# A ring of streamed expert weights: one matrix's slabs issued from ScalarE's queue instead of SyncE's

## Chip, cores and metric

One Trainium2 chip, one core. The metric is the device time of one execution in microseconds (us). Engines are named as in the profile: PE (TensorE), DVE (VectorE), ACT (ScalarE), POOL (GpSimd), SP (SyncE); an engine's name with q behind it is its sequencer.

## What is computed

The program computes two transformer blocks on 512 tokens of width 1024, all in float32. The first block (differential attention, a gated delta rule in both directions, then a mixture of experts) is followed by a second one of another kind. The change lies in the experts alone, which the reference gives as:

```python
def expert_choice_ffn(h, w_router, w_gate, w_up, w_down):   # 16 experts, width 2048
    cap = CAP_FACTOR * s // N_EXPERTS                        # 64 tokens for each expert
    aff = softmax(einsum('bsd,de->bse', h, w_router))
    top_val, top_idx = lax.top_k(swapaxes(aff, 1, 2), cap)
    xs = h[top_idx]
    gt = einsum('becd,edf->becf', xs, w_gate)
    up = einsum('becd,edf->becf', xs, w_up)
    ye = einsum('becf,efd->becd', silu(gt) * up, w_down)
    ye = ye * top_val[..., None]
    # scatter: every row of ye is added to its token's row of the output
```

Each of the three matrices of an expert has 2 million float32 values, 8 MB; the 16 experts' weights are 403 MB, each read once.

## The kernel before, in words

The weights of the experts go through a ring of 8 buffers (RING), each of 128 partitions by 4096 values, 2 MB. A load of one buffer is a slab. An expert x has PER = 12 slabs, numbered r = 12x to 12x + 11: four of w_gate, four of w_up, four of w_down ("down slabs"). Slab r goes to buffer r % 8. PE counts every slab that it has finished on the semaphore E7["used"]; slab r may be issued once used has reached r - 7, that is when slab r - 8 is finished. SP walks over all 192 slabs in order, waits for that count and issues one DMA for each (L1843 to L1854 with the helper expert_slab, whose plain issue is L1817; the slabs 8 to 11 go in two halves, L1814, and the last one, 191, in four quarters, L1821). All DMAs of the kernel are issued by SP.

PE runs the experts in order, two to a pair (L2081 to L2116). For each it does the gate slabs (wide(GB, ...), matmuls at L2048), in the second expert of a pair (odd x) four transposes (L2092), the up slabs (wide(UB, ...), L2048 too), the gather of the next pair's tokens (L2022), then turn (transposes, L2057) and two down slabs, turn and two more (down, L2077 and L2078). After the second expert of a pair comes the scatter: 8 products (L2115) that DVE adds to X (L2378). In the trace a slab is 16 matmul records, in pairs that run side by side on two halves of the array.

ACT does for each expert: two Silus of the gate's banks, which wait for used to reach 12x + 4 (L2186, L2187), the copy of the gathered tokens (L2178), and the two copies behind turn (L2192). DVE multiplies Silu by up (L2362), and copies the expert's output (L2367, L2368). Behind the stage, SP loads some constants for the next one (L1857 to L1864), each behind the buffer that it overwrites.

The loop of SP, cut:

```python
for r in range(NE * PER):
    ...
    elif r >= NR + 4:
        sp.wait_ge(E7["used"], r - NR + 1)
    expert_slab(sp, r)
```

Of the kernel before, what the change touches and what calls it, by code (L numbers as in the profile page):

```python
# [27 lines left out]
NE = 16  # L28
# [82 lines left out]
def build(nc, io):  # L111
    ctx = ExitStack()
    counts = {}
    with ctx:
# [5 lines left out]
        def sem(name):  # L120

            return cleared.pop(0) if cleared else ctx.enter_context(nc.semaphore(name))
# [87 lines left out]
        def load_slab(eng, slot, src, cols):  # L210

            k = src.shape[0] // P
            dst = SLB[slot][:, 0:k * cols].rearrange("p (k n) -> p k n", k=k)
            eng.dma_start(dst, src.rearrange("(k p) n -> p k n", p=P)).then_inc(slab_in[slot], 16)
            slab_n[slot] += 16
            return slab_in[slot], slab_n[slot]
# [938 lines left out]
        with nc.Block() as block:  # L1155
# [609 lines left out]
            E7 = {n: sem("e_" + n) for n in names}  # L1765
# [5 lines left out]
            NR = len(RING)  # L1771
            PER = 12
# [25 lines left out]
            def free_ring(eng, buf):  # L1798
                eng.wait_ge(E7["used"], max(r for r in range(NE * PER) if RING[r % NR] is buf) + 1)

            def expert_slab(eng, r):

                x, part = r // PER, r % PER
                if part < 8:
                    w, rows, f0 = (w_gate, w_up)[part // 4], 256, part % 4 * 256
                else:
                    w, rows, f0 = w_down, 512, DOWN[part - 8] * 512
                src = w[x, f0:f0 + rows, :].rearrange("(p k) n -> p (k n)", p=P)
                if NR <= r < NR + 4:

                    for k in range(2):
                        eng.wait_ge(*((E7["used"], r - NR + 1) if k else (E7["half"], r - NR + 1)))
                        cols = slice(k * 2 * D, (k + 1) * 2 * D)
                        eng.dma_start(RING[r % NR][:, cols], src[:, cols]).then_inc(ring_in[r % NR], 16)  # L1814
                    return
                if r < NE * PER - 1:
                    eng.dma_start(RING[r % NR][:, :], src).then_inc(ring_in[r % NR], 16)  # L1817
                    return

                for k in range(4):  # L1820
                    eng.dma_start(RING[r % NR][:, k * D:(k + 1) * D], src[:, k * D:(k + 1) * D]).then_inc(slab_in[4 + k], 16)  # L1821
                    slab_n[4 + k] += 16
                    quarter_in.append((slab_in[4 + k], slab_n[4 + k]))
# [3 lines left out]
            @block.sync  # L1827
            def _(sp):
                halves = lambda src, n: src[:, n * 512:(n + 1) * 512]
                sp.wait_ge(E4["o_done"], 2 * len(PAIRS))  # L1830
                sp.dma_start(wr, io["w_router"][0].rearrange("(k p) e -> p k e", p=P)).then_inc(E6["wr"], 16)
                for slot, src in ((5, halves(w_in[:, GATE_G:GATE_G + D], 1)), (6, halves(wpg, 0)), (4, halves(wpg, 1)),
                                  (0, halves(wo, 0)), (1, halves(wo, 1))):
                    if slot == 4:
                        sp.wait_ge(E4["sq4"], HEADS)
                    elif slot == 0:
                        sp.wait_ge(E4["og_ready"], HEADS)
                    elif slot == 1:
                        sp.wait_ge(q_done, 2 * SEVEN)
                    w5.append((slot, load_slab(sp, slot, src, 512)))  # L1840
                sp.dma_start(x3, io["x"][0].rearrange("(t p) d -> p t d", p=P)).then_inc(x_in, 16)

                for r in range(NE * PER):  # L1843
                    if r == 0:
                        sp.wait_ge(q_done, NQ * SEVEN)
                    elif r == 2:
                        sp.dma_start(n2row, io["norm2_w"].to_broadcast([P, D])).then_inc(E6["n2"], 16)
                    elif r == 4:
                        sp.wait_ge(merge5, KD)
                    elif r == 5:  # L1850
                        sp.wait_ge(m5, 2 * NT)
# [4 lines that stand above are left out]
                free_ring(sp, R[1])  # L1856
                sp.dma_start(nfrow, io["norm_f_w"].unsqueeze(0).to_broadcast([P, D])).then_inc(consts_in, 16)  # L1857
                sp.dma_start(onehot, io["table"][0:32, T_BUCKET:T_BUCKET + REL]).then_inc(consts_in, 16)
                sp.dma_start(rb, io["rel_bias_2"]).then_inc(consts_in, 16)
                sp.dma_start(kvrow, io["kv_norm_g_2"].to_broadcast([P, P])).then_inc(consts_in, 16)  # L1860
                sp.dma_start(w_uk, io["w_uk_2"][0].rearrange("h d r -> d h r")).then_inc(consts_in, 16)
                free_ring(sp, R[3])
                for to, c, n in ((0, A_CKV, P), (P, A_IK, 64), (P + 64, A_IW, 8)):
                    sp.dma_start(wm[:, :, to:to + n], w2[:, c:c + n].rearrange("(k p) n -> p k n", p=P)).then_inc(consts_in, 16)  # L1864
# [254 lines left out]
            def _(act):  # L2119
# [56 lines left out]
                def gathered(q, hf):  # L2176
                    act.wait_ge(E7["xg"], 2 * q + hf + 7)
                    nc.scalar.activation(XC[q % 2][:, 4 * hf:4 * hf + 4, :], OB[hf][:, :].rearrange("p (k n) -> p k n", k=4),  # L2178
                                         ACT.Copy).then_inc(E7["xc"], 1)
# [4 lines left out]
                for x in range(NE):  # L2184
                    for j in range(2):
                        act.wait_ge(E7["used"], PER * x + 4)  # L2186
                        nc.scalar.activation(SG[j], GB[j][:, :], ACT.Silu).then_inc(E7["silu"], 1)  # L2187
                    if x // 2 + 1 < NPAIR:
                        gathered(x // 2 + 1, x % 2)
                    for j in range(2):  # L2190
                        act.wait_ge(E7["tp_done"], 2 * x + j + 1)
                        nc.scalar.activation(HTE[:, 4 * j:4 * j + 4, :], TB[:, :].rearrange("p (c n) -> p c n", c=4), ACT.Copy)\  # L2192
                          .then_inc(E7["tp_evac"], 1)
# [209 lines left out]
            for i, (name, _) in enumerate(PROJ2):  # L2403
                UNITS += [(i, name, j) for j in range(4)]
            UNIT = {(name, j): n for n, (_, name, j) in enumerate(UNITS)}
            NS5 = 3
            FIRST = 4 * NS5
# [1005 lines left out]
```

## Time and profile before

| | |
|---|---|
| median of 3 runs | 2213.89 us (2213.62 to 2217.78) |
| the profiled execution | 2211.19 us, its span 2209.3 us |
| granted TensorE clock, mean | 0.993 |
| PE busy | 2061.1 us (93% of the span) |
| DVE, ACT, POOL busy | 903.9, 481.7, 230.1 us |
| bytes read from HBM | 494.62 MB |

The profile is of one execution. Times in it are microseconds from the start of the span. A line number is one of the kernel's source. "Idle before" is the time in which an engine stood still just ahead of the group's instructions, followed by what ended it. Matmul records overlap (they are pipelined, their ends are modelled), so a busy PE isn't a PE at its peak.

### The profile page before, as it was taken

To read this page: it belongs to the slowest core of one execution; us is meant where nothing else is said; L and a number is where in the kernel's file an instruction comes from. 1 tells how busy PE (TensorE), PEld (TensorE's weight loads), DVE (VectorE), ACT (ScalarE), POOL (GpSimd) and SP (SyncE) were. 2 spreads that over 40 slices of the span, in tenths; PEclk is the share of its full clock that TensorE was granted. 3 is DMA by queue.
4 is the path that set the end of the run, shared out by engine and by line. 5 is a ranking of instruction groups with operands and counts; after the bars stand their busy time and mean duration, and the time that the engine had idled before them with its cause. 6 is when DMAs were issued, how large, how long until landed. Compare 5 with 4: busy or idle time off the path is not lost. (4 is left out here: it accounts for less than half of the span.)

```text
span 2209.3 us, 25298 instructions
## 1 busy us (share of the span) xinstructions
PE 2061.1 (93%) x10306; PEld 1117.3 (51%) x10306; DVE 903.9 (41%) x1507; ACT 481.7 (22%) x879; POOL 230.1 (10%) x163
## 2 busy tenths in 40 slices
PE   8999999999999999799999898989898978999998
PEld 5885554445667785443433333333332325864444
DVE  2447767873556752401010100101010104796964
ACT  2445655412222510100000000000000002232333
POOL 1330000302333030000000000000000003221000
PEclk9999999999999999899999999999999999999999
DMA  7220111034222334499999999999999996311111
GB/s 263 77 82 36 39 39 27 20 94 120 77 71 83 116 115 200 153 398 428 428 427 427 429 427 428 428 427 427 428 427 429 427 428 252 101 58 58 62 58 38
DMA packets 112798, 499.99 MB, mean 226 GB/s; under 512 B 23530, under 2 KB 51208, under 8 KB 87468
## 3 DMA queue, kind: packets, MB, share of 16 engines
q1 hardware_dynamic: 112683, 498.39, 56.4%
q8 instruction: 82, 1.34, 0.2%
q14 instruction: 33, 0.26, 0.0%
HBM read 494.62 MB, written 5.06 MB: 226 GB/s over the span
## 5 line engine op out<-in xcount | busy, mean ns | idle before, releaser
L2048 PE MATMUL PS<-R 128*64 128x512 f32 x1024 | 232.1, 600 | 33.7 <-DMA R<-w_up 26.7
L2048 PE MATMUL PS<-SL,R 128*64 128x512 f32 x1024 | 228.9, 598 | 23.0 <-DMA SL<-w_gate 15.7
L2362 DVE TENSOR_TENSOR HT<-HT,PS 128x512 f32<-128x512 f32 x32 | 20.6, 684 | 369.4 <-PE PS L2048 369.4
L2048 PEld LDWEIGHTS PS<-R 128*64 128x64 f32 x1024 | 70.3, 137 | 184.0 <-issue 126.6
L2048 PEld LDWEIGHTS PS<-SL,R 128*64 128x64 f32 x1024 | 73.0, 137 | 176.1 <-issue 130.1
L2367 DVE COPY HT<-PS 64x512 f32<-64x512 f32 x16 | 10.9, 683 | 303.5 <-PE PS L2078 303.5
L2077 PE MATMUL PS<-SL,HT 128*64 128x512 f32 x256 | 114.4, 594 | 13.5 <-issue 6.0
L2077 PE MATMUL PS<-R,HT 128*64 128x512 f32 x256 | 114.3, 594 | 12.5 <-ACT HT L2192 7.0
L2078 PE MATMUL PS<-SL,HT 128*64 128x512 f32 x256 | 114.9, 596 | 0.0
L2078 PE MATMUL PS<-R,HT 128*64 128x512 f32 x256 | 114.8, 595 | 0.0
L1233 PE MATMUL PS<-HT,X 128*128 128x512 f32 x256 | 113.5, 595 | 0.0
L2528 POOL MEMSET SL<- 128x2048 f32 x1 | 1.8, 1804 | 1022.4 <-PE PS L2078 1022.4
L2187 ACT ACTIVATE HT<-PS 128x512 f32<-128x512 f32 x32 | 17.4, 594 | 414.6 <-PE PS L2048 414.6
L878 PE MATMUL PS<-HT,SL 128*128 128x512 f32 x240 | 105.6, 593 | 0.3 <-PEq L282 0.3
L2780 PE MATMUL PS<-HT,SL 128*128 128x512 f32 x192 | 84.7, 596 | 0.0
L1233 PEld LDWEIGHTS PS<-HT,X 128*128 128x128 f32 x256 | 47.6, 191 | 53.5 <-issue 53.3
L878 PEld LDWEIGHTS PS<-HT,SL 128*128 128x128 f32 x240 | 44.9, 190 | 54.2 <-issue 54.2
L2077 PEld LDWEIGHTS PS<-SL,HT 128*64 128x64 f32 x256 | 33.6, 137 | 74.6 <-issue 70.7
L2077 PEld LDWEIGHTS PS<-R,HT 128*64 128x64 f32 x256 | 33.6, 137 | 73.1 <-issue 70.3
L2178 ACT ACTIVATE R<-PS 128x512 f32<-128x512 f32 x14 | 8.4, 597 | 272.3 <-PE PS L2022 272.3
L2115 PE MATMUL PS<-HT,R 128*128 128x512 f32 x112 | 53.9, 618 | 10.4 <-DVE HT L2368 10.4
L628 PE MATMUL PS<-HT,SL 128*128 128x512 f32 x128 | 61.3, 612 | 0.0
(489 smaller groups left out, 3501.8 us busy)
## 6 DMA issues: line engine op xcount, KB each, us to landing
R<-w_gate SPq DMA_DIRECT2D x32, 2048.0 KB, 35.4
SL<-w_gate SPq DMA_DIRECT2D x32, 2048.0 KB, 33.6
SL<-w_up SPq DMA_DIRECT2D x32, 2048.0 KB, 32.6
R<-w_up SPq DMA_DIRECT2D x32, 2048.0 KB, 33.2
SL<-w_down SPq DMA_DIRECT2D x31, 2048.0 KB, 35.4
R<-w_down SPq DMA_DIRECT2D x28, 2048.0 KB, 27.8
SL<-w_in SPq DMA_DIRECT2D x18, 2048.0 KB, 7.9
SL<-grow SPq DMA_DIRECT2D x32, 256.0 KB, 4.8
```

The costliest lines, as they stand in the source:

```text
L628: m = pe.matmul(PS[5][:, :], slab(2 + f // 4)[:, k, f % 4 * P:(f % 4 + 1) * P], hT[:, k, :], start=(k == 0), stop=(k == KD - 1))
L878: m = pe.matmul(PS[n % 4][:, :], slab(i)[:, k, j * P:(j + 1) * P], hT[:, k, :], start=(k == 0), stop=(k == KD - 1))
L1233: m_ = pe.matmul(to[:, :], piece[m % 2][:, k, :], src[:, k, :], start=(k == order[0] and lo == 0), stop=(k == order[-1] and hi == KD))
L2048: m = pe.matmul(banks[n][half * CAP:(half + 1) * CAP, :], XC[x // 2 % 2][:, 2 * j + k, toks], w[:, k, (2 * half + n) * 512:(2 * half + n + ...
L2077: pe.matmul(DB[0:CAP, :], hk, w[:, k, 0:512], start=first, stop=last)
L2078: m = pe.matmul(DB[CAP:P, :], hk, w[:, k, 512:1024], start=first, stop=last)
L2115: pe.matmul(OB[half][:, :], STc[:, t, :], YP[:, half * 512:(half + 1) * 512], start=True, stop=True)\
L2178: nc.scalar.activation(XC[q % 2][:, 4 * hf:4 * hf + 4, :], OB[hf][:, :].rearrange("p (k n) -> p k n", k=4), ACT.Copy).then_inc(E7["xc"], 1)
L2187: nc.scalar.activation(SG[j], GB[j][:, :], ACT.Silu).then_inc(E7["silu"], 1)
L2362: tt(H[:, j, :], SG[j], UB[j][:, :], ALU.mult).then_inc(E7["h"], 1)
L2367: nc.vector.tensor_copy(YP[rows, 0:512], DB[0:CAP, :])
L2780: m = pe.matmul(bank_[:, :], slab(i % 2)[:, k, j * P:(j + 1) * P], hT[:, k, :], start=(k == 0), stop=(k == KD - 1))
```

## The change

ACT issues the down slabs of experts 1 to 15, except the very last slab, between its Silus and its copy of the gathered tokens. SP skips them. The wait for the buffer to be free stays the same. As ACT comes there only after used has reached 12x + 4, the wait for the buffers (12x + 1 to 12x + 4) is over by then.

```diff
+            def on_act(r):
+
+                return r >= PER and r % PER >= 8 and r < NE * PER - 1
+
             def expert_slab(eng, r):
...
                 for r in range(NE * PER):
+                    if on_act(r):
+                        continue
                     if r == 0:
...
                     for j in range(2):
                         act.wait_ge(E7["used"], PER * x + 4)
                         nc.scalar.activation(SG[j], GB[j][:, :], ACT.Silu).then_inc(E7["silu"], 1)
+                    for r in range(PER * x + 8, PER * x + 12):
+                        if on_act(r):
+                            act.wait_ge(E7["used"], r - NR + 1)
+                            expert_slab(act, r)
                     if x // 2 + 1 < NPAIR:
                         gathered(x // 2 + 1, x % 2)
```

## Rows read from the trace of the kernel before

**Rows 1.** The page: the span in 40 equal slices of 55.2 us.

```profile
DMA  7220111034222334499999999999999996311111
GB/s 263 77 82 36 39 39 27 20 94 120 77 71 83 116 115 200 153 398 428 428 427 427 429 427 428 428 427 427 428 427 429 427 428 252 101 58 58 62 58 38
```

**Rows 2.** Windows: us, busy by engine, granted clock, DMA share, GB/s.

```profile
1200.00:1810.00 610.00, 534.83 (x2458) 204.41 (x2456) 64.39 (x96) 27.19 (x49) 0.00 (x0) 0.99 1.01 428
```

**Rows 3.** Waits of PE from 1200 to 1810: us in total, times, longest.

```profile
PE PS L2048 <- DMA R<-w_up: 22.6, 20, 2.2
PE PS L2048 <- DMA SL<-w_gate: 15.7, 12, 2.0
...
PE PS L2077 <- DMA SL<-w_down: 1.0, 1, 1.0
```

**Rows 4.** Timeline, expert 15: start, us, engine, line, what, [idle before].

```profile
1807.14 3.65 PE L2048 MATMUL PS<-R 128*64 128x512 f32 x16 [1.23 <-DMA R<-w_gate]
...
1810.85 1.08 ACT L2187 ACTIVATE HT<-PS 128x512 f32<-128x512 f32 x2 [28.11 <-PE PS L2048]
...
1826.72 3.65 PE L2048 MATMUL PS<-SL,R 128*64 128x512 f32 x16 [1.23 <-DMA SL<-w_up]
...
1830.42 1.29 DVE L2362 TENSOR_TENSOR HT<-HT,PS 128x512 f32<-128x512 f32 x2 [18.31 <-PE PS L2048]
...
1832.65 0.61 PE L2077 MATMUL PS<-SL,HT 128*64 128x512 f32 x1 [0.73 <-issue]
...
1848.13 0.59 PE L2078 MATMUL PS<-R,HT 128*64 128x512 f32 x1
```

**Rows 5.** Timeline of PE in expert 1, three slabs lying ready.

```profile
985.57 10.50 PE L2048 MATMUL PS<-SL,R 128*64 128x512 f32 x48
995.87 3.63 PE L2048 MATMUL PS<-R 128*64 128x512 f32 x16
```

**Rows 6.** SP: issues; waits in all; L1817's issue to landing; that of 989.24.

```profile
989.24 7.19 SPq L1817 DMA_DIRECT2D SL<-w_down  x3
999.53 0.33 SPq L1817 DMA_DIRECT2D R<-w_down  x1
...
1022.85 8.87 SPq L1817 DMA_DIRECT2D SL<-w_up  x3
...
1130.71 8.87 SPq L1817 DMA_DIRECT2D SL<-w_up  x3
...
1248.83 8.87 SPq L1817 DMA_DIRECT2D SL<-w_up  x3
...
SPq L1817 <- PE PS L2048: 502.9, 119, 12.4
...
DMA to landing us min/median/max: 7.7/32.9/36.3
...
DMA to landing us min/median/max: 15.4/15.4/15.4
```

**Rows 7.** DMA queues from 1200 to 1700: packets, MB, share of 16 engines.

```profile
q1 hardware_dynamic: 14662, 213.57, 100.4%
q8 instruction: 16, 0.26, 0.2%
```

**Rows 8.** Timeline of PE: scatter of a pair, then the next gate slab.

```profile
1262.26 7.71 PE L2115 MATMUL PS<-HT,R 128*128 128x512 f32 x16 [1.49 <-DVE HT L2368]
1269.90 5.37 PE L2048 MATMUL PS<-R 128*64 128x512 f32 x24
```

**Rows 9.** Timeline of PE at three gaps; the granted clock (third from last) after one.

```profile
1207.09 8.78 PE L2048 MATMUL PS<-SL,R 128*64 128x512 f32 x32 [2.04 <-DMA SL<-w_gate]
1462.96 3.65 PE L2048 MATMUL PS<-R 128*64 128x512 f32 x16 [1.85 <-DMA R<-w_up]
1586.36 5.35 PE L2048 MATMUL PS<-R 128*64 128x512 f32 x16 [2.24 <-DMA R<-w_up]
1208.20:1211.70 3.50, 3.50 (x10) 0.93 (x8) 0.00 (x0) 0.00 (x0) 0.00 (x0) 0.53 1.03 440
```

## The prediction

> **What bounds the kernel now.** I read the page's slices first [rows 1]: from about 940 to 1840 us the DMA engines stand at 9 tenths or more with 427 to 429 GB/s in nearly every slice. This is the expert stage. A window over most of it [rows 2] gives a DMA share of 1.01, with PE busy for 535 of its 610 us and ACT for 27. The waits of PE [rows 3] say which of the two ends last: the largest are 22.6 us for up slabs and 15.7 for gate slabs, against 1.0 for down slabs. The timeline of one expert [rows 4] shows the pace: PE starts a slab every 4.895 us (four from 1807.14 to 1826.72), just after it landed, although the slab's work takes 3.43 us (three in 10.30 us where slabs lie ready [rows 5]). So the bytes bound this stage, and no order of issue can bring back more than such waits; what an order can do is to let the DMA engines run dry or to deliver the wrong slab first. SP's own issues [rows 6] repeat every 118.1 us for two experts (1130.71, 1248.83), against 24 x 4.895 = 117.5 us of transfer. PE alone would need 107.9 us for two (the same issue, an expert pair apart, while ready slabs still lay in the ring: 1022.85 and 1130.71).
>
> **What the change removes.** SP no longer issues 59 down slabs (four for each of experts 1 to 15, less the very last). An issue takes 0.33 us, and SP waits 503 us for PE at that same line [rows 6]: what SP saves is worth nothing. The Trainium skill says the same (DMA: Bandwidth & Descriptors, "Issuing engines are not separate DMA queues"): issuing from several engines saves the sequencer's time alone; by it the gain is 0.
>
> **What it adds on ACT.** Four waits and four issues, 1.3 us, behind two Silus of 1.08 us together [rows 4]. Behind them stands the copy of gathered tokens, which needs PE's gather over 14 us later (after four up slabs), so ACT's time costs nothing. No DMA of SP is moved past another one; the constants for the next stage stay behind SP's last slab.
>
> **What it moves.** Call T the end of an expert's fourth gate slab. Before, its four down slabs were issued as single slots came free, from 10 us ahead of T on: 989.24 to 999.53, with T at 999.5 [rows 6]. Now all four go out at T + 1.1 us. And they go into a second queue, while SP goes on with the next expert's gate slabs as soon as the first up slab is used. In the order of need this expert's down slabs come first; whether they come first now depends on how the 16 DMA engines share two queues. The trace has only one queue of slabs, so I bound it: at one end the transfers keep the order of issue, at the other one queue waits for the other. The nearest row is the instruction queue [rows 7]: in 500 us it got 16 packets through the same engines, 0.2% x 500 x 16 / 16 = 1.0 us for each, beside a slab queue that needs 33 to 36 us from issue to landing. A second queue is evidently not held behind the first one's backlog. Its packets (0.26 MB in 16) are like those of the slabs, 16 KB, so I take equal shares: a slab lands every 9.8 us from each while both have work. The Trainium skill has a rule for it (DMA: Bandwidth & Descriptors, "Queues, rings and completion order"): each engine goes round its queues, a packet from each; by it the shares are equal too, and no order of issue is kept.
>
> **The cycle with equal shares.** A slab issued to a quiet queue lands in 7.7 us [rows 6], so 2.8 us of lag and 4.9 of transfer. ACT's four (19.6 us of transfer) run from T + 3.9.
> - Even expert: SP's first new gate slab is issued at T + 3.4, runs from T + 6.2; until then ACT's have 2.3 us alone. The other 17.3 take 34.6, and SP has work all along. Last down slab lands at T + 40.8. PE has had nothing to do since it finished the one before (9.8 us spacing, 3.4 us of work: a gap of 6.4 us). It takes 3.4, then four gate slabs, long there, 13.7: next T after 57.9 us.
> - Odd expert: the 12 slabs of the cycle before (58.7 us) end 4.7 us after T (3.9 + 58.7 - 57.9), so up to T + 5.5 the queues share; four transposes (0.7) put SP's first issue later, 6.9. ACT has 2.2 us of work done by then, 17.4 x 2 = 34.8 left: T + 41.7. Then 3.4, the scatter of the pair 9.2 (from 1262.26 - 1.49 to 1269.90 [rows 8]) and 13.7: 68.0 us.
>
> Together 125.9 us for two experts against 118. PE sets this cycle with its wait for the last down slab, and in the odd one the DMA engines run dry before T. From T of expert 1 (999.5 [rows 6]) seven pairs lead to T of expert 15: 999.5 + 881.3 = 1880.8, against 1810.8 before [rows 4]: **+70.0 us**.
>
> **The clock.** PE's gaps before were 1.23 us in most slabs [rows 4]; the two longest, 2.04 and 2.24 us, were each followed by a stretch at half clock (granted 0.53, 1.2 instead of 2.4 GHz, for 3.5 us), a gap of 1.85 us was not [rows 9]. A slab cost 5.35 instead of 3.65 us there, **1.7 us** more. The gap of 6.4 us stands ahead of the last down slab, which is on the path: 14 x 1.7 = **+23.8 us**. The ends are 0 (the clock holds) and 48 (two such stretches each). The gap of some 3 us ahead of the third down slab costs nothing, as its loss falls into the next gap.
>
> **The end of the stage.** After T of expert 15 only four slabs are under way, three of ACT and SP's last: all land by T + 23.5, so PE isn't held: 0.7 and 13.7 for the up slabs, 2.2 for DVE's product, turn and ACT's copy (1830.42 to 1832.65), 16.1 for the down slabs (to 1848.7): 32.7 us, against 38.0 (1810.8 to 1848.7), all [rows 4]: **-5.3 us**. Behind it nothing changes.
>
> **Sum:** 70.0 + 23.8 - 5.3 = +88.5. The profiled execution was 2211.2 us (1.9 above its span of 2209.3), so it would be 2299.7; the median of the runs is 2.7 us above it: **2302 us**, 4.0% slower. With the clock's ends it is 2278 to 2327.
>
> **Rivals.**
> 1. *Transfers keep the order of issue* (nearly no change). While the stage is bound by bytes, at T the fifth slab is just arriving and three and a fraction more are queued, 16 us of work, against a delay of 3.9: never dry. Only at expert 1, when PE runs on a stock, does it show: the first down slab on the path landed at 989.24 + 15.4 = 1004.6 [rows 6]; now it would land at 1000.6 + 7.7 = 1008.3. The delay of 3.7 us is never won back, and may occur twice while the stock lasts: +4 to +8, 2218 to 2222 us. Against it: the instruction queue. Chance 0.12.
> 2. *ACT's queue gets more than half.* At 60% the last down slab of an even expert lands at T + 35, but 12 slabs need 58.7 us anyway; the odd one needs 68.0 - 5.8 = 62.2. Seven pairs of 120.9 put T of expert 15 at 1845.8, +35; less 5.3, and up to 12 for the clock: +30 to +42, 2244 to 2256 us. Chance 0.10.
> 3. *SP's queue gets more* (40% for ACT: 17.3 / 0.4 is 8.7 us more than 17.3 / 0.5, in 14 cycles +122: 2424 us). Nothing speaks for it but that SP's slabs are ahead in every engine. Chance 0.08.
> 4. *Faster: two queues fill gaps between packets.* Place: the DMA engines' rate. 184 slabs x 4.895 = 901 us go at that pace, so 1% more rate is 9 us. It needs the order of issue kept as well (it pays that case's 4 to 8 us), so it decides from 0.8% on; at 2% it is -11: 2203 us. Against it: a share of 1.01 leaves no gaps [rows 2]. Chance 0.06.
> 5. *The change doesn't do what it says*: if ACT's issues took far longer than SP's 0.33 us, ACT would come late to the evacuations; at 2 us each it still isn't, so this has no case of its own.
>
> **Numbers.** Equal shares 0.64. Its own range is 2270 to 2335. The whole range goes down to the case of kept order and up past the clock's end: 2217 to 2350. A measurement of this kernel tells about 0.2% (4.4 us) from no change. Faster 0.06; same 0.08 (most of rival 1 lies just above the bound); slower 0.86.
>
> **What would show it.** Issue to landing of ACT's down slabs near 10, 20, 30 and 40 us, 9.8 apart; PE's waits moved from gate and up slabs to down slabs, the longest near 6 us, some 15 of them; a pair in 126 to 130 us; a DMA share under 1 in some windows; granted clock under 1 once per expert. Down slabs landing 4.9 us apart would refute equal shares; a pair under 119 us would refute the forecast altogether.

## The result, and the profile after

| | before | after |
|---|---|---|
| median (4 runs each) | 2213.76 us | 2285.07 us (2283.35 to 2290.84) |
| span of the profiled execution | 2209.3 us | 2284.1 us |
| ratio, 95% interval | | 1.033 (1.0318 to 1.0343) |

The change makes the kernel 71 us slower. The forecast was 2302 us, 88 us slower; 2285 lies inside its range (2217 to 2350) and inside that of equal shares (2270 to 2335). The page of the changed kernel, its slices and its queues (each slice is 57.1 us), beside [rows 1] and [rows 7]:

```profile
PEclk9999999999999999999989998999999889999999
DMA  7230111143222434798989989898989998121210
GB/s 255 74 113 1 38 38 34 32 118 95 75 75 82 165 140 168 275 396 375 426 346 425 424 369 427 344 424 363 427 359 428 390 385 308 60 94 37 79 56 37
q1 hardware_dynamic: 104187, 374.65, 41.6%
q10 hardware_dynamic: 8496, 123.74, 13.1%
```

The second queue is there (q10, 59 slabs of ACT). In the expert stage nearly every other slice has fallen from 428 to between 344 and 396 GB/s. In nearly the same stretch as before, the windows show it as a DMA share of 0.95 where it was 1.01 [rows 2], and a granted clock of 0.93 where it was 0.99:

```profile
1200.00:1800.00 600.00, 512.43 (x2292) 197.96 (x2288) 56.10 (x84) 26.60 (x48) 0.00 (x0) 0.93 0.95 400
```

PE's waits from 1000 to 1880 us (in us in total, times, longest) have changed sides. There is none left for gate or up slabs [rows 3], and 104.5 us for down slabs:

```profile
PE PS L2083 <- DMA SL<-w_down: 56.0, 13, 6.8
PE PS L2083 <- DMA R<-w_down: 48.5, 14, 6.1
```

One cycle in the timeline, from T of expert 6 (1319.7) to T of expert 7 (1378.0). L2083 and L2084 are the down slabs, L2054 gate and up slabs:

```profile
1319.79 0.60 ACT L2193 ACTIVATE HT<-PS 128x512 f32<-128x512 f32 x1 [39.70 <-PE PS L2054]
1319.80 0.82 ACTq L1821 DMA_DIRECT2D R<-w_down  x2
1320.28 0.59 ACT L2193 ACTIVATE HT<-PS 128x512 f32<-128x512 f32 x1
...
1338.66 0.61 PE L2083 MATMUL PS<-R,HT 128*64 128x512 f32 x1 [0.75 <-issue]
...
1347.93 0.64 PE L2083 MATMUL PS<-R,HT 128*64 128x512 f32 x1 [1.50 <-DMA R<-w_down]
...
1357.73 1.11 PE L2083 MATMUL PS<-SL,HT 128*64 128x512 f32 x1 [6.14 <-DMA SL<-w_down]
...
1364.10 10.47 PE L2054 MATMUL PS<-SL,R 128*64 128x512 f32 x48
1374.40 3.60 PE L2054 MATMUL PS<-R 128*64 128x512 f32 x16
1377.93 0.66 PE L2098 MATMUL PS<-tab,R 128*128 128x128 f32 x4
```

The reader should see four things. The third and the last down slab start 9.80 us apart, twice the 4.9 us of a transfer; issue to landing of the four was 8.2, 17.6, 27.2 and 36.5 us, where I forecast about 10, 20, 30 and 40. PE stands still for 6.14 us ahead of the last one. That slab then takes 6.37 us (1357.73 to 1364.10) with matmuls of 1.11 us instead of 0.6. And the four gate slabs behind it lay ready: no wait ahead of them. The queues from 1330 to 1354 us (packets, MB, share of 16 engines) say why it is 9.80:

```profile
q10 hardware_dynamic: 351, 5.23, 51.1%
q1 hardware_dynamic: 343, 5.10, 49.7%
```

Equal shares, within 3%. In a window at the end of an odd expert's cycle, just before T of expert 6, the engines move nothing (DMA share 0.00, the second number from the end), and one over the last down slab has the clock at 0.57:

```profile
1357.50:1364.50 7.00, 6.77 (x18) 2.00 (x20) 0.18 (x1) 0.00 (x0) 0.00 (x0) 0.57 1.03 440
1313.60:1319.50 5.90, 5.90 (x30) 1.98 (x28) 0.00 (x0) 0.00 (x0) 0.00 (x0) 1.00 0.00 0
```

Measured from the same trace, the 14 cycles from T of expert 1 (998.1) to T of expert 15 (1890.3) take 892.2 us, against 811.3 before (999.5 to 1810.8); even cycles 58.6 us on average, odd ones 68.9.

### The profile page after: what moved, and what is told of

It reads as the page before. It is cut to its first block and busy times, and to the rows that moved or that the text cites. A ratio compares the mean times of both kernels' runs of the same rounds, so it can differ in the third digit from the quotient of the medians.

```text
span 2284.1 us, 25298 instructions
## 1 busy us (share of the span) xinstructions
PE 2099.6 (92%) x10306; PEld 1124.0 (49%) x10306; DVE 903.2 (40%) x1507; ACT 481.9 (21%) x879; POOL 230.2 (10%) x163
## 5 line engine op out<-in xcount | busy, mean ns | idle before, releaser
L2054 PE MATMUL PS<-R 128*64 128x512 f32 x1024 | 227.1, 594 | 0.0
L2054 PE MATMUL PS<-SL,R 128*64 128x512 f32 x1024 | 223.9, 592 | 0.0
L2083 PE MATMUL PS<-SL,HT 128*64 128x512 f32 x256 | 144.1, 721 | 63.6 <-DMA SL<-w_down 56.0
L2083 PE MATMUL PS<-R,HT 128*64 128x512 f32 x256 | 136.4, 689 | 55.3 <-DMA R<-w_down 48.5
L2054 PEld LDWEIGHTS PS<-SL,R 128*64 128x64 f32 x1024 | 73.6, 137 | 146.2 <-issue 146.1
L2084 PE MATMUL PS<-SL,HT 128*64 128x512 f32 x256 | 144.3, 722 | 0.0
L2054 PEld LDWEIGHTS PS<-R 128*64 128x64 f32 x1024 | 71.7, 137 | 141.5 <-issue 140.8
L2084 PE MATMUL PS<-R,HT 128*64 128x512 f32 x256 | 136.6, 689 | 0.0
L2083 PEld LDWEIGHTS PS<-SL,HT 128*64 128x64 f32 x256 | 40.0, 165 | 151.0 <-issue 86.2
L2083 PEld LDWEIGHTS PS<-R,HT 128*64 128x64 f32 x256 | 38.1, 157 | 136.6 <-issue 79.8
L2028 PEld LDWEIGHTS PS<-R 128*128 128x128 f32 x448 | 53.8, 196 | 11.4 <-issue 11.4
```

Source lines behind the costliest of these rows:

```text
L2028: m = pe.matmul(OB[hf][:, c * P:(c + 1) * P], h2[:, t, 256 * j + k:256 * (j + 1):2], Sel[q % 2][:, t, :], start=(t == 0), stop=(t == NT - 1))
L2054: m = pe.matmul(banks[n][half * CAP:(half + 1) * CAP, :], XC[x // 2 % 2][:, 2 * j + k, toks], w[:, k, (2 * half + n) * 512:(2 * half + n + ...
L2083: pe.matmul(DB[0:CAP, :], hk, w[:, k, 0:512], start=first, stop=last)
L2084: m = pe.matmul(DB[CAP:P, :], hk, w[:, k, 512:1024], start=first, stop=last)
```

## Experiments

Each ran beside the kernel before on the same chip; ratios are to it. The medians of the kernel before in these sets were 2212.24 to 2213.61 us, so a difference of mine to the changed kernel, which ran in another set, is good to some 2 us beside the scatter. The first four take the change apart: is it the late issue, the second queue, or the two together?

**Late, but in one queue (e1).** To the kernel before:

```diff
+                    elif r >= PER and r % PER >= 8 and r < NE * PER - 1:
+                        sp.wait_ge(E7["used"], r // PER * PER + 4)
                     elif r >= NR + 4:
```

> All DMAs on SP as before, but SP holds the four down slabs of experts 1 to 15 (not the very last slab) until the fourth gate slab is used, which is when ACT issued them in the changed kernel. One queue keeps the order of issue. My theory (the loss comes from two queues sharing the engines equally while the needed slabs are also late): the queue still holds four up slabs at that time, so it hardly runs dry; only while PE works on its stock does it lose once or twice: +4 to +8 us on the kernel before, 2218 to 2222 us. Rival A (the late issue alone does it, the queue is of no matter): as the changed kernel, 2270 to 2290 us.

Measured: 2216.66 us (10 runs; before 2213.61), ratio 1.0018 (1.0009 to 1.0028): +3 us. PE's waits from 1000 to 1860 us are for gate and up slabs as before, none for down slabs, and the DMA share stays 1.01. The two largest:

```profile
PE PS L2050 <- DMA R<-w_up: 28.4, 26, 1.3
PE PS L2050 <- DMA SL<-w_gate: 17.0, 15, 1.3
```

And the window from 1200 to 1800 us:

```profile
1200.00:1800.00 600.00, 525.54 (x2428) 201.63 (x2424) 64.41 (x96) 27.19 (x49) 0.00 (x0) 1.00 1.01 428
```

The late issue alone costs next to nothing: rival A falls. The four up slabs still in the queue cover it, as the share of 1.01 shows.

**Two queues, but prompt (e2).** ACT's four issues stand ahead of its Silus:

```diff
                 for x in range(NE):
+                    for r in range(PER * x + 8, PER * x + 12):
+                        if on_act(r):
+                            act.wait_ge(E7["used"], r - NR + 1)
+                            expert_slab(act, r)
                     for j in range(2):
                         act.wait_ge(E7["used"], PER * x + 4)
...
-                    for r in range(PER * x + 8, PER * x + 12):
```

> The changed kernel, but ACT issues its four down slabs ahead of its Silus, each as soon as its buffer is free, as SP did before. So two queues without the late issue. My theory: with equal shares the down slabs now delay the up slabs that are needed first, PE waits for up slabs, but all four down slabs are in when it gets to them and the engines never run dry: +8 to +18 us on the kernel before, 2222 to 2232 us. Rival A (lateness alone): 2214 us. Rival B (any use of a second queue costs what was measured): 2270 to 2290 us.

Measured: 2228.74 us, ratio 1.0079 (1.0057 to 1.01): +15 us. The engines stay busy (1.00), but PE now waits up to 6.2 us for up slabs, since the down slabs take half of the engines while the up slabs are due (waits from 1000 to 1860 us):

```profile
PE PS L2054 <- DMA SL<-w_up: 30.4, 7, 6.2
PE PS L2054 <- DMA R<-w_up: 28.3, 8, 6.1
```

And the window from 1200 to 1800 us:

```profile
1200.00:1800.00 600.00, 536.04 (x2454) 215.50 (x2452) 63.04 (x94) 27.79 (x50) 0.00 (x0) 0.97 1.00 427
```

T of expert 15 comes only 3.6 us later than before (1814.4 against 1810.8); 9 us are lost behind it (47.0 instead of 37.9 us to the last down slab), where the last expert's up slabs share the engines with slabs that are needed after them. So 3 us for being late, 15 for the down slabs in a second queue, and 71 for both.

**Every other slab on ACT (e4).** Two queues, with each slab issued when it is due:

```diff
-                return r >= PER and r % PER >= 8 and r < NE * PER - 1
+                return r >= PER and r % 2 == 1 and r < NE * PER - 1
...
+                def act_slabs(upto):
+                    while todo and todo[0] - NR + 1 <= upto:
+                        r = todo.pop(0)
+                        act.wait_ge(E7["used"], r - NR + 1)
+                        expert_slab(act, r)
```

(todo holds ACT's slabs in order; act_slabs is called ahead of the Silus, behind them, and behind each of the two copies at the expert's end, with the count of used slabs that is reached there anyway: 12x + 4, + 8, + 10, + 12.)

> Every odd slab from 13 on (but 191) is issued by ACT, each as soon as its buffer is free as far as ACT's other work lets it, every even one by SP: two queues whose heads are always the next two slabs that PE needs. My theory (it is the order of need against equal shares that costs, not the second queue): +0 to +5 us on the kernel before, 2214 to 2219 us. Rival B (a second queue costs by itself): over 2225 us. Rival C (two queues fill gaps between packets and raise the rate by 1%): 2205 us.

Measured: 2214.96 us (10 runs), ratio 1.0006 (0.9996 to 1.0015). No difference from the kernel before. The queues from 1200 to 1700 us:

```profile
q10 hardware_dynamic: 7332, 106.76, 50.2%
q1 hardware_dynamic: 7332, 106.79, 50.2%
```

213.55 MB in all, against 213.57 in one queue [rows 7]. A second queue costs nothing by itself, if its head is the slab that is needed next or next but one, and brings no rate either, which also settles my rival 4 (faster).

**SP's next gate slabs held back (e5).** To the changed kernel, only waits are added:

```diff
+                    elif r >= 2 * PER and r % PER < 4:
+                        sp.wait_ge(E7["used"], (r // PER - 1) * PER + 8)
                     elif r >= NR + 4:
```

> The changed kernel, but SP holds the next expert's four gate slabs back until the eighth slab (the last up slab) of this expert is used, some 14 us after ACT has issued its down slabs. It only adds waits. My theory (SP's gate slabs, which nobody needs for another 40 us, take half of the engines from the down slabs that are needed next): the down slabs land some 5 us apart as long as SP is held, the last one by about T + 28 instead of T + 39 (T: the fourth gate slab used), PE no longer waits for it; the price is that the gate and up slabs come later and PE waits for up slabs in every other expert: worked through with the intervals of the changed kernel's trace, 2250 to 2268 us, 17 to 35 us FASTER than the changed kernel. Rival A (the down slabs are slow because they are issued late, whoever else is there): an added wait can't help, 2285 us or more.

Measured: 2257.48 us, ratio 1.02 (1.0177 to 1.0223): 28 us faster than the changed kernel by doing nothing but wait. The last packet of ACT's four slabs starts on average 27 us after an even T in place of 37. PE's waits from 1000 to 1860 us:

```profile
PE PS L2056 <- DMA R<-w_up: 51.5, 14, 6.2
PE PS L2056 <- DMA SL<-w_up: 21.6, 6, 4.1
PE PS L2085 <- DMA SL<-w_down: 1.4, 1, 1.4
```

The waits for down slabs are gone (1.4 us instead of 104.5), and 73.1 us have come back as waits for up slabs, with a DMA share of 0.97 from 1200 to 1800 us. This is the clearest sign that it was the slabs needed latest that held up those needed first.

**Only the third and fourth down slab on ACT (e6).** The condition of on_act is r % PER >= 10 instead of 8.

> The changed kernel with only the third and fourth down slab of an expert on ACT, issued after the Silus as there; SP issues the other two when their buffers are free. The third is then 3.4 us later than in the kernel before and the fourth not late at all; both are in the second queue. My theory: half the number of slabs against SP's queue, so the fourth lands at about T + 22, long before PE needs it at T + 31; the up slabs lose some turns: +2 to +8 us on the kernel before, 2216 to 2222 us, so the cost is no fixed price for each slab on ACT. Rival B (a fixed price for each slab issued by ACT, 71 us / 59): +35 us, 2248 us.

Measured: 2219.26 us (10 runs; before 2212.24), ratio 1.0029 (1.0019 to 1.0038): +7 us for 29 slabs, where all 59 cost 71. No price by the slab. In this trace the last packet of ACT's slabs starts at T + 23 on average (in the changed kernel at T + 37 in even experts), and PE, which wants the last down slab from T + 31 on, never waits for one. What is left are waits for up slabs from 1000 to 1860 us, as in the run with prompt issues (e2):

```profile
PE PS L2054 <- DMA R<-w_up: 28.3, 6, 6.1
PE PS L2054 <- DMA SL<-w_up: 25.6, 6, 6.1
```

**The clock (e3).** My forecast had 23.8 us for half clock behind PE's gap. This run fills a part of that gap with matmuls of no use:

```diff
                         down(x, 2)
+                        if 0 < x < NE - 1:
+                            warm_up(pe, 16, PS[0][:, 0:P])
                         down(x, 3)
```

> The changed kernel with 16 small transposes of the identity by itself (128x128, into the first gate bank, which is free then; some 3.5 us) ahead of the last down slab of experts 1 to 14, that is inside the gap of 6 us in which PE waits for it. If the half clock after that gap is a term of its own (last down slab 6.1 us instead of 3.4), these slabs get back to 3.4 to 4 us and the time falls by up to 14 x 2.7 = 38 us: 2247 to 2265 us. Rival (the slab is slow for another reason, or the clock falls whatever PE does in a part of the gap): no gain, 2280 to 2290 us.

Measured: 2276.7 us, ratio 1.0289 (1.0269 to 1.0308): 8 us less than the changed kernel, between the two expectations: a miss of both. The timeline of expert 6 (the last down slab again):

```profile
1351.00 3.84 PE L194 MATMUL PS<-tab 128*128 128x128 f32 x32
1357.40 0.64 PE L2083 MATMUL PS<-SL,HT 128*64 128x512 f32 x1 [2.56 <-DMA SL<-w_down]
...
1360.89 1.46 PE L2054 MATMUL PS<-SL,R 128*64 128x512 f32 x6
```

It takes 3.49 us now, not 6.37, so the clock is what made it slow; even cycles fell from 58.6 to 56.1 us. But odd ones didn't (69.6, before 68.9). I first took this for the third slab, which in odd experts is slow as well (the gap ahead of it was 5.1 to 6.6 us in six of the seven odd experts, more than the 3 us that I wrote in the expectation):

> As the run with small matmuls in the gap before the last down slab (e3), and in odd experts 12 more ahead of the third down slab, where the trace of e3 shows that the clock had fallen already in the gap of 3 us before the third, so that this slab took 6 us and the later matmuls no longer fitted. If that is why e3 brought 8 us and not 38, the odd cycles now shorten by 2.5 us as the even ones did: 2248 to 2262 us. Rival (in the odd cycles something else is last): 2273 to 2280 us, as e3.

(This is e7: 12 more warm_up matmuls ahead of down(x, 2) for odd x.) Measured: 2276.42 us, ratio 1.0292 (1.0273 to 1.031). A miss; it came out as the rival. Nearly all slabs ran at full clock in this trace (17 us of half clock from T of expert 1 to T of expert 15 instead of 130), and the odd cycles still took 69.2 us: their last down slab was 2.3 us quicker but came 2.6 us later. The engines have 12 slabs = 58.7 us of work for each cycle; an even cycle that lasts 56 us leaves the rest to the odd one, at the worst time. Two runs (e8 and e9) test that, with the matmuls in odd experts alone (12 ahead of the third, 16 ahead of the last slab) and in even experts alone (16 ahead of the last):

> As the run before (small matmuls in the gaps ahead of the third and the last down slab), but in odd experts alone. My theory of why that run brought only 8 us: the engines need 58.7 us for the 12 slabs of a cycle, so what an even cycle gains below that is left over at the odd expert's T as up slabs of SP, which hold ACT's down slabs back by as much (first packet at T + 3.5 instead of T + 2, last landing 2.4 us later in the trace). With even cycles left slow, the odd ones should keep their whole gain: 7 x 2.7 = 19 us less than the changed kernel, 2263 to 2270 us. Rival (the small matmuls in odd experts bring nothing, since something else is last there): 2280 us or more.

> Small matmuls ahead of the last down slab in even experts alone. By the same theory the even cycles shorten by 2.5 us each and the odd ones lengthen by as much: no gain, 2281 to 2288 us. Rival (each gap's clock loss is a term of its own, as my prediction had it): 7 x 2.5 = 17 us less than the changed kernel, 2268 us.

Measured: odd alone 2272.97 us, ratio 1.0273 (1.0259 to 1.0287), 12 us less than the changed kernel. That is at least as much as with both (the intervals of the two ratios overlap), although the even cycles kept their half clock. It falls short of the 19 that I expected, between the two expectations: the slow clock costs an odd expert's last slab 2.3 us on average, not 2.7, and two of the seven were still slow (5.2 us). Even alone 2289.19 us, ratio 1.0347 (1.0332 to 1.0361): no gain, 1 us above my range. Its even cycles took 55.8 us (2.8 less), its odd ones 71.7 (2.8 more). The queues in the 3.5 us from T of expert 7, first in the changed kernel (1378.0 to 1381.5), then in this one (1381.5 to 1385.0):

```profile
q1 hardware_dynamic: 72, 0.95, 64.0%
q10 hardware_dynamic: 29, 0.48, 34.0%
```

```profile
q1 hardware_dynamic: 94, 1.46, 98.5%
q10 hardware_dynamic: 1, 0.02, 1.1%
```

What the even cycle gained stands ahead of ACT's slabs as leftover up slabs: 1.46 MB of SP's instead of 0.95, and one packet of ACT's instead of 29.

No run points to a version that beats the kernel before. With the DMA share at 1.01 there, an order of issue can at best keep the stage's time.

## Why the prediction was right, and where it was off

**Shown as forecast.** The bytes bound the stage, and the change turned it into one that PE's wait for the last down slab bounds (waits, cycle above). Shares are equal (351 to 343 packets). SP's saved issues and ACT's added ones are worth nothing. ACT's issues were at times far longer than 0.33 us, up to 2.21 us in odd experts, but the copy behind turn came 18.9 us after the first Silu there, as where they were short:

```profile
1122.50 0.60 ACT L2193 ACTIVATE HT<-PS 128x512 f32<-128x512 f32 x1 [31.04 <-PE PS L2054]
1123.37 2.21 ACTq L1821 DMA_DIRECT2D SL<-w_down  x1
1141.42 0.59 ACT L2202 ACTIVATE HT<-PS 128x512 f32<-128x512 f32 x1
```

A pair was to take 126 to 130 us; it took 124.4 to 129.9. The end of the stage took 32.4 us (forecast 32.7) instead of 37.9. T of expert 15 was forecast at 1904.6 (1880.8 and the 23.8 of the clock) and came at 1890.3 (ACT's first Silu behind it starts at 1890.30). Of the 14.3 us between, 1.4 stand before T of expert 1; the rest is seven pairs of 127.5 us, where the sum with the clock had 129.3. Two errors of mine lie in that, the start of ACT's transfers and the clock's price.

**Off: the start of ACT's transfers** ("from T + 3.9"). I put 1.1 us for two Silus and 2.8 of lag. The rows above show the first issue at 1319.80, beside the first Silu, 0.1 us after T; its first packet is at T + 1.0. So the last down slab of an even expert starts at T + 38.5 on average, not 40.8, and that of an odd one at T + 39.8, not 41.7: 4.2 us less for a pair.

**Off: the clock's price** ("1.7 us more", "14 x 1.7 = +23.8"). Its size for one slab was too small, and I counted it too often. The last down slab of an even expert takes 6.1 us on average where it takes 3.4 at full clock: it loses 2.7 us, not 1.7. That of an odd one loses 2.3 (7.4 us to the first product of the scatter, instead of 5.1). From its start to the next T it takes 1.3 us longer than in my sum in an even cycle and 1.0 in an odd one: 2.3 us more for a pair, against the 4.2 less above. That the forecast is only 17 us off is in part owed to these two working against each other. And I took the clock's loss for a term of its own in each cycle. Even cycles were at 57.9 in my own sum, under the engines' 58.7, so what the clock takes there comes out of a leftover that would have hurt the next cycle. The pair of runs with odd or even experts alone shows that: 12 us and none. Taking the half clock away brought 9 us (both) or 12 (odd alone) of the 71 by the medians, and 15 or 14 between the T of experts 1 and 15 in the profiled executions, where I had 24. The leftover of bytes was in my sum for the odd cycle, but I didn't work it out again after I had made the even cycle longer by the clock.

**The rivals.** Kept order (1) came true in the run where one queue keeps it: +3 us, where I had 4 to 8. Unequal shares (2, 3), a higher rate (4) and late evacuations (5) are refuted by the rows. The range (2217 to 2350) was wide because equal shares rested on one row of the instruction queue; that reading held.

## What to carry to other kernels

A queue is an order. As long as a stage is bound by bytes, one queue delivers what is needed next and a moderate delay of an issue costs little (3 us here); splitting the stream by matrix over two queues gives half of the engines to whatever stands at the head of the other, also to slabs that nobody needs for 40 us. If two engines must issue, split so that the two heads are always the next two in the order of need. And when a term is added to one cycle of an alternating pair, put the bytes through both cycles again before multiplying by their number.

## What the runs showed of the hardware beyond what I expected

- ACT's DMA issues don't wait for the activations ahead of them: the first issue is at 1319.80, the Silus at 1319.79 and 1320.28, although both stand ahead of it in the program. The issue's own wait, for used, was over by then. It was so, 0.01 us behind the first Silu's start, for all experts from 1 to 14.
- The first packet of ACT's queue starts 1.0 us after T where the engines are idle and 3.4 to 3.6 us after T where SP's queue has work for that long (e9, odd experts from 3 to 13), so a newcomer isn't in the round at once. In expert 7 of that run 65 large packets of SP start in the 2.5 us between, some four on each of the 16 engines (0.62 us each). Once both are in, the shares are equal (351 to 343, above).
- Waiting can pay: the changed kernel with nothing but one more wait for four DMAs of each expert (e5) was 28 us faster than without it.
